# Five residual chunks in place of three for GpSimd, three in place of five for VectorE

## The reference

```
x = x + gate * rmsnorm(y, g)        # y is what the sublayer made
h = rmsnorm(x, g_next) * ... + ...  # the next sublayer's input
```

## Time and profile before

| | |
|---|---|
| median of 3 runs | 2156.29 us (2156.28 to 2158.05) |
| profiled execution, its own time | 2157.66 us |
| profiled execution, its span | 2155.8 us |
| mean granted TensorE clock in it | 0.992 |
| busy: PE, DVE, POOL, ACT | 97%, 52%, 45%, 41% |

### The profile page before, as it was taken

One profiled execution on the slowest core, in us unless ns is written; L12 is line 12 of the kernel. 1 busy time (PEld: TensorE's weight loads), 2 busy tenths in 40 slices (PEclk: granted clock), 3 DMA queues, 4 the chain that ended last, 5 costly groups with the idle time before them and its releaser, 6 DMA issues.

```text
span 2155.8 us, 28064 instructions
## 1 busy us (share of the span) xinstructions
PE 2084.8 (97%) x9946; PEld 1695.1 (79%) x9946; DVE 1122.4 (52%) x1749; ACT 876.4 (41%) x1490; POOL 968.6 (45%) x489
## 2 busy tenths in 40 slices
PE   8999999989999999999999999999999999999997
PEld 5777787878888888787768788888777788888887
DVE  3535744335577776764474543434575525434335
ACT  4226864445222222533475422333465534323233
POOL 3436885433355444433233344444435633444443
PEclk9999999999999999999999999999999999999999
DMA  5440052214466664274002233333222012333332
GB/s 180 166 141 7 21 205 89 78 31 156 139 233 214 229 234 141 91 250 138 20 1 93 78 94 94 97 96 97 82 85 69 1 59 79 98 92 95 96 97 88
DMA packets 67925, 234.47 MB, mean 109 GB/s; under 512 B 7296, under 2 KB 10752, under 8 KB 67712
## 3 DMA queue, kind: packets, MB, share of 16 engines
q1 hardware_dynamic: 67840, 233.33, 33.1%
HBM read 231.20 MB, written 2.10 MB: 108 GB/s over the span
## 4 chain that ended last, share of the span: by engine, by line
PE 60%; issue 20%; POOL 9%; DVE 5%; ACT 4%; DMA 1%; POOLq 0%; SPq 0%; DVEq 0%; ACTq 0%
PE bank L906 18%; PE bank L908 18%; PE bank L907 18%; POOL WL L768 6%; PE bank L1003 1%; PE bank L1018 1%; POOL sq L822 1%; PE bank L1127 1%; DMA stage<-panels 1%; POOL t L822 1%; DVE acc L2309 0%; PE bank L1198 0%; PE bank L1500 0%; PE bank L1232 0%; ACT WH L1603 0%
## 5 line engine op out<-in xcount | busy, mean ns | idle before, releaser
L768 POOL TENSOR_TENSOR WL<-stage,WH 128x1024 fp32r<-128x1024 f32 x264 | 657.2, 2491 | 928.7 <-ACT WH L1603 928.5
L1603 ACT ACTIVATE WH<-stage 128x1024 fp32r<-128x1024 f32 x264 | 279.9, 1060 | 829.7 <-PE bank L908 775.9
L906 PE MATMUL bank<-H,WH 128*128 128x512 f32 (+1 forms) x1196 | 465.4, 389 | 18.8 <-POOL WL L768 10.9
L907 PE MATMUL bank<-H,WH 128*128 128x512 f32 (+1 forms) x1196 | 463.4, 387 | 0.0
L908 PE MATMUL bank<-H,WL 128*128 128x512 f32 (+1 forms) x1196 | 463.3, 387 | 0.0
L906 PEld LDWEIGHTS bank<-H,WH 128*128 128x128 f32 x1196 | 225.5, 189 | 70.2 <-issue 15.7
L2663 DVE TENSOR_TENSOR Y<-bank,Y 128x512 f32<-128x512 f32 x328 | 215.8, 684 | 94.7 <-PE bank L908 94.0
L906 PE MATMUL bank<-HID,WH 128*128 128x512 f32 (+1 forms) x688 | 264.3, 384 | 0.1
L907 PE MATMUL bank<-HID,WH 128*128 128x512 f32 (+1 forms) x688 | 264.2, 384 | 0.0
L908 PE MATMUL bank<-HID,WL 128*128 128x512 f32 (+1 forms) x688 | 264.2, 384 | 0.0
L907 PEld LDWEIGHTS bank<-H,WH 128*128 128x128 f32 x1196 | 225.6, 189 | 45.8 <-issue 0.5
(11 more groups left out here) (447 smaller groups left out, 3551.5 us busy)
## 6 DMA issues: line engine op xcount, KB each, us to landing
stage<-panels SPq DMA_DIRECT2D x296, 512.0 KB, 3.6
ahead<-ada SPq DMA_DIRECT2D x96, 512.0 KB, 5.3
RAW<-panels SPq DMA_DIRECT2D x18, 512.0 KB, 4.1
apiece<-ada SPq DMA_DIRECT2D x16, 512.0 KB, 3.7
x<-xT SPq DMA_DIRECT2D x3, 1024.0 KB, 8.2
outT<-x SPq DMA_DIRECT2D x16, 128.0 KB, 1.7
x<-xT SPq DMA_DIRECT2D x2, 512.0 KB, 4.4
Y<-bias SPq DMA_DIRECT2D x1, 1024.0 KB, 5.7
```

Source lines behind the costliest of these rows:

```text
L768: pool.tensor_tensor(low_of(p, slot), stage[:, slot, :], high_of(p, slot).bitcast(F32), ALU.subtract).then_inc(s_split, 1)
L906: pe.matmul(out, wh, rh, start=start, stop=False)
L907: pe.matmul(out, wh, rl, start=False, stop=False)
L1603: act.activation(high_of(p, slot), stage[:, slot, :], ACT.Copy).then_inc(s_hisplit, 1)
```

## The change

`POOL_ADDS`, the list of chunks that GpSimd adds in every residual, goes from (1, 3, 5) to (0, 2, 3, 5, 6). VectorE keeps chunks 1, 4 and 7. The count of VectorE's adds is now worked out from the list, where 5 and 13 stood. The number of multiplies is the same (8 for each residual, or 16 halves), and each chunk of x is still added once.

```diff
-POOL_ADDS = (1, 3, 5)
+POOL_ADDS = (0, 2, 3, 5, 6)
...
         def added_before(name):
 
-            return sum(13 if other in HALVED else 5 for other in RESID[:RESID.index(name)])
+            by_vector = KC - len(POOL_ADDS)
+            return sum(KC + by_vector if other in HALVED else by_vector for other in RESID[:RESID.index(name)])
```

## The result

The changed kernel takes 2164.91 us (median of 8 runs, 2162.06 to 2168.07), the kernel before 2156.64 (8 runs, 2154.09 to 2160.82): a ratio of 1.0037, 95% interval 1.0026 to 1.0047. It is slower by 8.3 us, where 1.5 was forecast and 2160.5 was the upper end. The profiled execution took 2165.11 us, with a span of 2163.3. Lines of the source are one higher now (L789 adds, L769 splits).

A forecast was written before the change was run, and what follows sets the result against it. TensorE, busy 97% of 2155.8 us, was taken as the bound, so other engines count only where it waits. Terms +0.2 + 1.2 + 0.35 - 0.2 = +1.5 us on a median of 2156.29 gave 2157.8 us, range 2154.0 to 2160.5.

The forecast's parts named there:

- the sum: Whole kernel: +0.2 (ffn, mlp0), +1.2 (ca, a, b), +0.35 (mix) and -0.2 (end) add up to +1.5 us.
- Whole residuals: At ffn and mlp0, chunk 0 comes 0.09 later and starts the row of sums later: +0.09 each, +0.2 together.
- the pace of the two buffers: At ffn and mlp0, two buffers of squares going back and forth set the pace; the row of sums stays 7.67 long.
- `ca`, `a`, `b`: Half-width residuals: GpSimd's adds end later and the feed-forward starts later, +0.39 each, +1.2 together.
- The end of GpSimd's adds: At ca, a and b, GpSimd's last add ends 4.31 after the first multiply, where it was 3.91.
- The chain over the split and the DMA: At ca, a and b, GpSimd's adds delay a panel's split, then a DMA, ScalarE's rounding and TensorE's start.
- `mix`: Residual where VectorE also adds squares: its last add of squares ends behind GpSimd's second split, +0.35.
- up to 361.72 nothing moves: At mix, nothing shifts until 361.72, as GpSimd's third add ends where its second did.
- The +0.5: Cost of mix, in place of +0.35, if the skill's port rule blocks GpSimd's add of chunk 6 until 363.1.
- The end: After the last residual only stores follow, issued in order; they are done earlier: -0.2.
- VectorE as the bound: Rival: VectorE bounds the residuals, gaining 1.1 per whole and 0.54 per half one, 5.5 in all: 2150.8 us; chance 0.03.
- The stretch of GpSimd's adds: Rival: close-standing adds each let a multiply pass, adding 2.4 at ca, a and b: +8.7, 2165.0 us; chance 0.04.

The follow-up runs named there:

- e12: Changed kernel with 8 filler matmuls in TensorE's idle stretch at mix and 8 more behind the sums of ca, a and b: ratio 1.0017 to the kernel before.
- e10: Kernel before with GpSimd adding the five chunks at ffn and mlp0 alone: ratio 0.9995, -0.5 us.
- e8: Kernel before with GpSimd adding the five chunks at ca, a and b alone: ratio 1.0016, +2.7 us.
- e7: Kernel before with GpSimd splitting the next panel ahead of its adds at ca, a and b: ratio 0.9997, -1.4 us.
- e11: Kernel before with VectorE adding all eight chunks at ca, a and b, GpSimd none: ratio 0.9997, +0.1 us.
- e3: Changed kernel with 8 filler matmuls in TensorE's idle stretch at mix: ratio 1.0023 to the kernel before, +6.0 us.
- e4: Kernel before with 8 filler matmuls in TensorE's idle stretch at mix: ratio 1.0007, +1.7 us.
- e9: Kernel before with 10 more filler matmuls behind mix, everything later put off by 2.2 us: ratio 1.0028, +7.3 us.
- e13: Kernel before with 5 more filler matmuls behind mix, everything later put off by 1.1 us: ratio 1.0024, +6.0 us.
- e14: Kernel before with 15 more filler matmuls behind mix, everything later put off by 3.4 us: ratio 1.0007, +3.6 us.
- e15: Changed kernel with 8 filler matmuls in the idle stretch at mix and 12 more (2.7 us) behind it: ratio 1.0032 to the kernel before, +8.0 us.
- e2: Kernel before with GpSimd adding the five chunks at all residuals but mix: ratio 1.0002, +0.3 us.

## Why the prediction was wrong

*The step that failed is the sum.* It took the four kinds of places, and added them up as if the 2,000 us between them would stay as long as they were. They did not: about 4.4 us of the loss is TensorE at its lower level for longer. In part that is at `mix` and behind `ca`, where the longer idle stretches were followed by a fall of 1.6 us each; by e12, more of it lies in stages that the change doesn't touch. The profile before had the hint, a mean clock of 0.992 and not 1.000, and idle stretches in the attentions with 0.83 and 0.95 around them; the prediction had no term for it and no rival. The bound of what can be told, 0.2%, was taken for noise to both sides. It is mostly this clock: the runs of the kernel before spread from 2152.6 to 2168.2 us, and a rest of 1.2 us remains once the clock is taken out.

*The steps themselves held in the main.*
- Whole residuals: +0.13 and +0.12 in the trace for 0.09 each; the pace of the two buffers, not VectorE (e10, the row of sums at 7.67 and 7.68).
- `ca`, `a`, `b`: +0.22, +0.20 and +0.08 in the changed kernel's trace, +0.36, +0.36 and +0.29 over eight traces against seven, +1.2 at equal clock in e8, for 1.2. The 0.3 behind `ca`, in the feed-forward, comes on top. The end of GpSimd's adds was right to 0.01. The chain over the split and the DMA is shown by e7 and e11, which move it.
- `mix`: 0.66 (e3 against e4) for 0.35. The last add of squares ended behind the second split, as foretold, and the lengths were right too: GpSimd's add took 1.68 (1.7 foretold), its splits 2.81 each (about 2.8). What failed is "up to 361.72 nothing moves": the first add of squares took 0.84 longer beside GpSimd's three adds, and the end of the second comes 8.20 after the first multiply (361.02 + 1.42 - 354.24), for 7.95 before (361.72 - 353.77). All that follows is later by this 0.25. The Trainium skill (SBUF — State Buffer, Who interferes with whom) lets the later of two such instructions wait for the whole of the other. The trace agrees to 0.13: GpSimd's add, at 363.30, met VectorE's, which ended at 363.81, and itself ended 1.17 later (364.98), where it takes 1.30 alone. The +0.5 that the prediction drew from this rule is nearer, but by luck, since the rest came from the earlier add.
- The end: -0.21 for -0.2 (eight stores issued in 3.87 for 4.16).
- Together 0.66 + 1.01 + 0.25 - 0.21 = 1.7 us from the traces, against 1.5, and 2.0 with the 0.3 behind `ca`. At equal clock the runs say 2.6, give or take 0.8, so no more than chance is between them (a slope of 2.16 us for 0.001, an estimate of what a TensorE that is always the bound would lose, 2157 us x 0.001, makes it 1.8).

*The rivals.* VectorE as the bound fell (e10, e11). The stretch of GpSimd's adds fell at half width: their median is 0.736. It gave the right size of the time, 2165.0, by luck: by a mechanism that isn't there.

*What stays open* is at which moments the clock is granted and taken, and so whether 1.1 and 2.2 us are bad shifts and 3.4 isn't, as the means of e9, e13 and e14 have it and e15 doesn't. No version beat both kernels by more than can be told: e7 (0.9997) and e11 (0.9997) equal the kernel before, and are faster than the changed one.

## What to carry to other kernels

Before summing waits, look at the mean granted clock and at the stretches where it isn't 1.00: where it is not, a shift of a microsecond or two can cost several (1.1 and 2.2 us cost 6.0 and 7.3 here), in stages far behind the change, and a small forecast needs that in its range. To tell the two apart, compare times at equal clock over many runs, run a kernel that is only shifted, and keep a second trace of each kernel: what differs between two traces of one kernel is no effect of the change. And an engine that is half idle can still be dear: GpSimd's adds stood ahead of a panel's split, and the split ahead of a DMA that the next stage began with.

## What was not expected of the hardware

- A mere shift, 2.2 us of TensorE's own filler matmuls, made the kernel 7.3 us slower by the medians, and one of 3.4 us made it 3.6 us slower.
- 128x512 matmuls of the sums take 1.10 for a pair at 2.4 GHz and 2.05 at 1.2 GHz right after 2.34 us of idle time; after 1.75 us at the same place in the kernel before the clock did not fall. In e2 it did, after 1.9, with `mix` unchanged.
- Two instructions of VectorE and GpSimd that both read two tiles of SBUF delay each other to both sides: the add of squares took 4.95 for two behind two splits, and the splits 5.62 for two, where about 4.8 is usual.
